# The order of VectorE's and ScalarE's steps in the projection and attention stages of a one-core encoder block

## The chip, the cores and the metric

The kernel runs on one core of a Trainium2 chip. The metric is device time in microseconds (us), the median of several runs. The core has five engines with a queue of instructions each: TensorE (PE; its weight loads are PEld), VectorE (DVE), ScalarE (ACT), GpSimd (POOL) and SyncE (SP, which issues most of the transfers). Each engine works through its own queue in the order of the program; the engines wait for one another through semaphores.

## The reference, cut to what matters

One layer of an encoder with 512 tokens and a width of 1024, in three residual blocks. Only the first block is touched by the change:

```python
xn = rms_norm(h, mix_norm[l])
q_a, k_a, v_a, q_b, k_b, v_b, q_i, k_i, w_i = jnp.split(xn @ w_in[l], IN_SPLITS, axis=-1)
# branch A: p = softmax of 4 heads x 2 maps; a = p[:, :, 0] - lam * p[:, :, 1]; o = a @ v
y_a = diff_attention(q_a, k_a, v_a, lam, slopes_a)
# branch B: isc = sum over 4 heads of relu(q_i k_i) * w_i; the 128 best keys of each query (top_k);
# softmax over these, 8 heads with one shared k_b, v_b
y_b = dsa_attention(q_b, k_b, v_b, q_i, k_i, w_i * ..., slopes_b, k_sel)
gates = jax.nn.sigmoid(xn @ w_gate[l] + b_gate[l])
h = h + (g_a * (y_a @ w_branch_a[l]) + g_b * (y_b @ w_branch_b[l])) @ w_out[l]
```

Behind it come cross attention over 256 memory tokens and a mixture of 32 experts, 2 for each token, whose weights are the larger part of all bytes that are read.

## The kernel before, in words

All five engines walk one list, `steps`, written out by hand near line 330; for each step an engine issues what that step gives it, and nothing if the step gives it nothing. Moving a step in the list moves its instructions in every engine's queue.

**Weights.** A weight matrix comes in chunks of at most 128x2048 numbers into a ring of three buffers `raw`. The step `("split", n)` turns chunk n into two parts: ACT copies it to `whi` (L904) once the chunk has landed and once PE has finished with chunk n-2, whose buffer it takes; DVE then writes the low part `wlo` = `raw` - `whi` (L1222). SP loads chunk n+3 when that low part is written. A step `("fm", n, j)` multiplies one half j of a chunk: 24 matmuls of 128x512 (L1647 to L1649: high x high, low x high, high x low, eight k). It waits for the low part of its chunk. Chunk 0 holds the keys of branch B and of the index (`CH_K`), chunk 1 `v_b` and `w_i` (`CH_VBWI`, 24 matmuls in the step `("vbwi",)`), chunk 2 the index queries (`CH_QI`). After `("fm", CH_K, 0)` ACT copies the keys out of PSUM (`kbT` L926, `kiT` L927) and issues two small transfers that double them to the other half of the partitions (L929, L930). The first reader of the doubled keys is the first step `("index", 1, 0)`, L1811 on PE.

**Selection.** The 128 best keys of each query come from 16 rounds for each of the query tiles 1, 2 and 3: a step `("topk", qt, r)` is one MAX (L1252) and one MATCH_REPLACE (L1253) on DVE. `select(n)` puts the next n of these steps into the list. Tile 3 must be through before unit 28 of the attention is scored.

**Attention.** Branch A is 16 units (4 query tiles x 4 heads), branch B 16 more (4 query tiles x 4 pairs of heads), 32 in all, u = 0 to 31. Each unit u has these steps:
- `("score", u)`: PE multiplies queries and keys (L1824), DVE adds the distance term (L1271) and takes the row maximum (L1273), for both maps;
- `("exp", u)`: ACT, softmax numerator and its sum (L976);
- `("fin", u)`: in branch A three instructions on DVE (L1282, L1283, L1286) that divide by the sums and subtract the two maps; in branch B one reciprocal on DVE (L1289) and two scalings on ACT (L984);
- `("tr", u)`: PE transposes the result (L1832), after waiting for `fin` of u; ACT copies it out of PSUM (L993);
- `("av", u)`: PE multiplies with the values (L1845 in branch A, L1850 in B); ACT and, in branch B, DVE copy out.

The loop over u puts down, for each u: `tr(u)`, `fin(u+1)`, `score(u+3)`, `exp(u+2)`, a `split` where u is a positive multiple of 4, twelve matmuls of a gate projection (`fm_half` or `fm`), `av(u)`, and perhaps `select(1)`. Ahead of the loop stand the two chunks `CH_QB` (the queries of branch B, chunks 9 and 10), with `fin(0)` and four selections each. PSUM has eight banks that are filled in turn; a step that fills a bank waits until the one before it is copied out.

Of the kernel before, what the change touches and what calls it, by code (L numbers as in the profile page):

```python
# [10 lines left out]
TT = SEQ // P  # L11
# [30 lines left out]
def build(nc, x, mem, mix_norm, w_in, lam_q1, lam_k1, lam_q2, lam_k2, diff_subln, w_branch_a, w_branch_b,  # L42
# [13 lines left out]
    def at(name, shape, dtype, start, offset=0):  # L56
        return nc.alloc_sbuf_tensor_at(name, shape, dtype, offset=start + offset)
# [33 lines left out]
    vbwi = at("vbwi", [DH_B + H_I, SEQ], f32, R_B)  # L91
# [177 lines left out]
    def fm_chunk(src, c0):  # L269

        chunks.append((256, [(src[:, :, c0:c0 + 256], 0, KT, 0, 256)]))
        return len(chunks) - 1
# [9 lines left out]
    CH_K = 0  # L282
    chunks.append((68, [(win[:, :, C_VB:C_VB + 64], 0, KT, 0, 64), (win[:, :, C_WI:C_WI + 4], 0, KT, 64, 4)]))
    CH_VBWI = 1
# [4 lines left out]
    CH_QB = [fm_chunk(win, C_QB + 256 * j) for j in (0, 1)]  # L289
# [25 lines left out]
    A_UNITS = [("A", qt, hd) for qt in range(TT) for hd in range(H_A)]  # L315
    B_UNITS = [("B", qt, pair) for qt in range(TT) for pair in range(H_B // 2)]
    UNITS = A_UNITS + B_UNITS
    steps = [("norm", "x"), ("cols",), ("split", 0)]
    steps += [("xT", k) for k in range(KT)] + [("split", 1)]

    def fm(n, js=(0, 1)):
        for j in js:
            steps.append(("fm", n, j))
        if n + 2 < NCH:
            steps.append(("split", n + 2))
# [7 lines left out]
        if n + 3 < NCH:  # L333
            steps.append(("split", n + 3))

    fm(CH_K, (0,))
    steps.append(("vbwi",))
    steps.append(("split", CH_VBWI + 2))
    steps += [("fm", CH_QI, 0), ("vbwiT",), ("fm", CH_QI, 1), ("split", CH_QI + 2), ("lambda",)]

    selecting = [("index", qt, hd) for qt in range(1, TT) for hd in range(H_I)]
# [2 lines left out]
    def select(n=2):  # L344
        steps.extend(selecting[:n])
        del selecting[:n]
# [14 lines left out]
    for n in CH_QB:  # L361
        steps.append(("fm", n, 0))
        if n == CH_QB[1]:
            steps.append(("fin", 0))
        select(2)
        steps.append(("fm", n, 1))
        steps.append(("split", n + 2))
        select(2)

    gate_tiles = [(CH_G[g // 2], g % 2) for g in range(2 * KT)]  # L370
    for u in range(len(UNITS)):
        steps.append(("tr", u))
        if u + 1 < len(UNITS):
            steps.append(("fin", u + 1))
        if u + 3 < len(UNITS):
            _, qt, _ = UNITS[u + 3]
            assert not any(q <= qt for _, q, _ in selecting) or UNITS[u + 3][0] == "A"
            steps.append(("score", u + 3))
        if u + 2 < len(UNITS):
            steps.append(("exp", u + 2))  # L380
        if u % 4 == 0 and u:
            steps.append(("split", CH_G[u // 4 - 1] + 2))
        if u < 2 * len(gate_tiles):
            n, j = gate_tiles[u // 2]
            steps.append(("fm" if u % 2 else "fm_half", n, j))
        steps.append(("av", u))
        if u < 2 * TT or u >= len(A_UNITS):
            select(1)
        if u == len(UNITS) - 2:

            steps.append(("yanorm",))
    n = CH_BR[0]
# [9 lines left out]
    n = CH_WO[1]  # L402
# [9 lines left out]
    n = CH_CV[1]  # L412
# [5 lines left out]
    for hx in range(1, H_X):  # L418
        n = CH_CQ[hx]
# [7 lines left out]
    n = CH_CO[0]  # L427
# [9 lines left out]
    steps = [s for s in steps if s[0] != "split" or s[1] < NCH]  # L437
# [10 lines left out]
    for s in steps:  # L448
# [15 lines left out]
        elif kind in ("score", "tr"):  # L464
            u = UNITS[s[1]]
# [1691 lines left out]
```

## Time and profile before

| | us |
|---|---|
| median of 3 runs | 1059.52 |
| lowest and highest | 1059.39, 1059.64 |
| the profiled execution's own time | 1057.06 |
| its span in the profile | 1055.3 |
| PE busy | 998.5 (95%) |
| DVE busy | 503.1 (48%) |
| ACT busy | 342.9 (32%) |
| PE's part of the chain that ended last | 80% |

The first stage (projections, both attentions, the gates) ends near 300 us, the cross attention near 560 us, the routing of the experts near 590 us; the experts take the rest. A row of the timeline has: start, duration, engine, line, operation, out<-in, shape, and in brackets the idle time of that engine before it with what ended it. Starts and durations are in us. The durations of instructions that follow one another overlap, so the pace of an engine is read from starts. ACTq and SPq are the engines' issues of transfers.

### The profile page before, as it was taken

The numbers are of one execution on the slowest core, as the hardware profiler recorded it, in microseconds if no ns is written. First come the engines' busy times: TensorE is split into PE (matmuls) and PEld (weight loads), VectorE is DVE, ScalarE is ACT, GpSimd is POOL, SyncE is SP. The second block draws the span as 40 slices with busy tenths as digits, with TensorE's granted clock in tenths as the row PEclk, the third lists the DMA queues.
The fourth block names the chain that finished last, engine by engine and source line by source line (L and its number), as shares of the span: only waits on it lengthen the run. The fifth ranks groups of instructions, "written<-read, shape, count | busy, mean of one in ns | idle before, by whom it ended". The sixth has DMA issues, their size and how long they took to land.

```text
span 1055.3 us, 12594 instructions
## 1 busy us (share of the span) xinstructions
PE 998.5 (95%) x4901; PEld 628.9 (60%) x4901; DVE 503.1 (48%) x915; ACT 342.9 (32%) x684; POOL 41.9 (4%) x59
## 2 busy tenths in 40 slices
PE   8999989989999999999997999999999889898894
PEld 6778857766778889887786444344443333333342
DVE  4369799766557545433336433333332232333236
ACT  6342346667872335443323211111111110111113
POOL 1000000000000000000000100000000000000001
PEclk9999999999999999999997999999999999999997
DMA  8322311211213525421287999999999999999992
GB/s 244 121 81 80 114 46 41 80 40 44 78 40 104 216 82 198 160 80 40 101 325 319 346 429 427 426 424 428 427 424 427 427 427 427 427 427 427 427 407 93
DMA packets 64431, 260.72 MB, mean 247 GB/s; under 512 B 11329, under 2 KB 39026, under 8 KB 50802
## 3 DMA queue, kind: packets, MB, share of 16 engines
q1 hardware_dynamic: 59954, 248.08, 59.3%
q0 software_dynamic: 3104, 7.35, 1.9%
q10 hardware_dynamic: 1312, 4.46, 1.1%
q8 instruction: 41, 0.67, 0.3%
q14 instruction: 20, 0.16, 0.0%
HBM read 259.60 MB, written 4.19 MB: 250 GB/s over the span
## 4 chain that ended last, share of the span: by engine, by line
PE 80%; DMA 13%; DVE 2%; issue 2%; ACT 2%; SPq 0%; DVEq 0%; ACTq 0%
PE ps L1956 16%; PE ps L1647 13%; PE ps L1649 13%; PE ps L1648 13%; DMA eraw<-in_w 12%; PE ps L2009 8%; PE ps L2020 2%; PE ps L1824 2%; PE ps L2021 2%; PE ps L1832 1%; PE ps L1882 1%; PE ps L1904 1%; PE ps L1850 1%; PE ps L1845 1%; PE ps L1943 1%
## 5 line engine op out<-in xcount | busy, mean ns | idle before, releaser
L1956 PE MATMUL ps<-eraw,XT 128*64 128x512 f32 x992 | 225.9, 598 | 12.8 <-DMA eraw<-in_w 11.6
L1222 DVE TENSOR_TENSOR wlo<-raw,whi 128x2048 fp32r<-128x2048 f32 (+2 forms) x43 | 95.9, 2230 | 120.0 <-ACT whi L904 119.8
L1956 PEld LDWEIGHTS ps<-eraw,XT 128*64 128x64 f32 x992 | 67.4, 137 | 133.6 <-issue 129.4
L2009 PE MATMUL ps<-eraw,HT 128*64 128x512 f32 x512 | 113.0, 594 | 8.0 <-issue 8.0
L1516 DVE TENSOR_TENSOR h<-ps,h 128x512 f32<-128x512 f32 x128 | 79.4, 682 | 82.9 <-PE ps L2021 82.9
L1647 PE MATMUL ps<-xT_hi,whi 128*128 128x512 f32 (+1 forms) x256 | 104.8, 409 | 2.8 <-DVE xT_lo L1229 1.6
L1648 PE MATMUL ps<-xT_lo,whi 128*128 128x512 f32 (+1 forms) x256 | 100.4, 392 | 0.0
L1649 PE MATMUL ps<-xT_hi,wlo 128*128 128x512 f32 (+1 forms) x256 | 100.2, 392 | 0.0
L904 ACT ACTIVATE whi<-raw 128x2048 fp32r<-128x2048 f32 (+2 forms) x43 | 80.1, 1863 | 44.7 <-PE ps L1649 43.2
L2009 PEld LDWEIGHTS ps<-eraw,HT 128*64 128x64 f32 x512 | 39.4, 137 | 79.7 <-issue 79.7
L1062 ACT ACTIVATE HT<-ps 128x512 f32<-128x512 f32 x15 | 9.0, 597 | 197.7 <-PE ps L1994 197.7
L1508 DVE TENSOR_TENSOR Yl<-ps,Yh 128x512 fp32r<-128x512 f32 x32 | 22.1, 691 | 96.7 <-ACT Yh L1081 96.7
L1647 PEld LDWEIGHTS ps<-xT_hi,whi 128*128 128x128 f32 (+1 forms) x256 | 47.9, 187 | 28.6 <-issue 15.0
L1525 DVE TENSOR_TENSOR gg<-ps,sg 128x512 f32<-128x512 f32 x16 | 11.1, 691 | 96.5 <-ACT sg L1090 94.5
L1649 PEld LDWEIGHTS ps<-xT_hi,wlo 128*128 128x128 f32 (+1 forms) x256 | 47.8, 187 | 11.0
L2020 PE MATMUL ps<-Yh,S 128*128 128x512 f32 x128 | 53.7, 420 | 0.3 <-DVE Yl L1508 0.3
L1648 PEld LDWEIGHTS ps<-xT_lo,whi 128*128 128x128 f32 (+1 forms) x256 | 48.1, 188 | 9.2
L1081 ACT ACTIVATE Yh<-ps 128x512 fp32r<-128x512 f32 x32 | 19.1, 597 | 100.7 <-PE ps L2009 100.7
L2021 PE MATMUL ps<-Yl,S 128*128 128x512 f32 x128 | 50.4, 394 | 0.0
L2020 PEld LDWEIGHTS ps<-Yh,S 128*128 128x128 f32 x128 | 24.0, 187 | 28.9 <-issue 23.9
L976 ACT ACTIVATE s<-s,nmax 128x128 f32<-128x128 f32 (+3 forms) x64 | 35.4, 560 | 1.0 <-DVE nmax L1273 0.6
L1090 ACT ACTIVATE sg<-ps 128x512 f32<-128x512 f32 x16 | 9.6, 597 | 77.0 <-PE ps L1956 77.0
(316 smaller groups left out, 1576.0 us busy)
## 6 DMA issues: line engine op xcount, KB each, us to landing
eraw<-in_w SPq DMA_DIRECT2D x82, 2048.0 KB, 29.1
eraw<-in_w SPq DMA_DIRECT2D x28, 1024.0 KB, 11.2
raw<-in_w_in SPq DMA_DIRECT2D x9, 1024.0 KB, 5.3
raw<-in_w_gate SPq DMA_DIRECT2D x8, 1024.0 KB, 5.4
raw<-in_w_ckv SPq DMA_DIRECT2D x8, 1024.0 KB, 5.2
raw<-in_w_out SPq DMA_DIRECT2D x4, 1024.0 KB, 5.0
raw<-in_w_cq SPq DMA_DIRECT2D x4, 1024.0 KB, 5.1
raw<-in_w_co SPq DMA_DIRECT2D x4, 1024.0 KB, 4.9
```

Source lines behind the costliest of these rows:

```text
L904: act.activation(whi[n % 2][:, 0:w], raw[n % RING][:, 0:w], ACT.Copy).then_inc(w_hi, 1)
L976: act.activation(b, b, ACT.Exp, bias=nmax[:, u % 3, m:m + 1], accum_out=ssum[:, u % 3, m:m + 1]).then_inc(exp_done, 1)
L1222: dve.tensor_tensor(wlo[n % 2][:, 0:w], raw[n % RING][:, 0:w], whi[n % 2][:, 0:w].bitcast(f32), ALU.subtract).then_inc(w_lo, 1)
L1508: dve.tensor_tensor(Yl[:, c], ps[4 + n][:, :], Yh[:, c].bitcast(f32), ALU.subtract).then_inc(yl_kept, 1)
L1516: dve.tensor_tensor(v, ps[bank][:, :], v, ALU.add).then_inc(comb_added, 1)
L1647: pe.matmul(o, ahi, bhi, start=start, stop=False)
L1648: pe.matmul(o, ahi, blo, start=False, stop=False)
L1649: return pe.matmul(o, alo, bhi, start=False, stop=stop)
L1956: ins = pe.matmul(ps[1 + c // 2][rows, :], XT[p % 2][:, kk, rows], eraw[slot][:, first + 512 * k:first + 512 * k + 512], start=(kk == 0), ...
L2009: ins = pe.matmul(ps[4 + n][rows, :], HT[:, ff, rows], eraw[slot][:, first + D * f + 512 * n:first + D * f + 512 * n + 512], start=(ff == ...
L2020: pe.matmul(o, S[:, P * t:P * t + P], Yh[:, c], start=True, stop=False)
L2021: pe.matmul(o, S[:, P * t:P * t + P], Yl[:, c], start=False, stop=True).then_inc(comb_made, 1)
```

## The change

Three things are edited in `steps`; no instruction is added or removed, and the memory layout is as before.

1. `("split", 2)` moves ahead of `("fm", CH_K, 0)`. (`CH_K + 2` and `CH_VBWI + 1` are both chunk 2; `CH_VBWI + 2`, chunk 3, stays behind `vbwi`.)
2. `("fin", 1)` moves from the loop's first pass to the chunk `CH_QB[1]`, behind its second half and ahead of `("split", 12)`.
3. The loop's `select(1)` used to stand in the units 0 to 7 and from 16 on. Now it stands in units that are no multiple of 4, up to 11 and from 16 on. The 11 rounds that are left for the loop (5 to 15 of tile 3) were in the units 0 to 7 and 16 to 18; they are now in 1, 2, 3, 5, 6, 7, 9, 10, 11, 17 and 18.

```diff
-    fm(CH_K, (0,))
-    steps.append(("vbwi",))
-    steps.append(("split", CH_VBWI + 2))
+
+    steps += [("split", CH_K + 2), ("fm", CH_K, 0), ("vbwi",), ("split", CH_VBWI + 2)]
...
         steps.append(("fm", n, 1))
+        if n == CH_QB[1]:
+            steps.append(("fin", 1))
         steps.append(("split", n + 2))
...
         steps.append(("tr", u))
-        if u + 1 < len(UNITS):
+        if 0 < u < len(UNITS) - 1:
             steps.append(("fin", u + 1))
...
         steps.append(("av", u))
-        if u < 2 * TT or u >= len(A_UNITS):
+
+        if u % 4 and (u < 3 * TT or u >= len(A_UNITS)):
             select(1)
```

On PE, POOL and SP no instruction changes its place. From here on the changed kernel's lines are 2 higher.

ACT's queue at the start of the projections, before: the keys (`kbT`, `kiT`) and their two transfers stand ahead of the copy of chunk 2 (`raw2` to `whi0`).

```order
L904 ACTIVATE whi1_53<-raw1_50 128x544
L926 ACTIVATE kbT_83<-ps1 64x512
L927 ACTIVATE kiT_84<-ps1 64x512
L929 DMA kiT_84<-kiT_84 64x512
L930 DMA kbT_83<-kbT_83 64x512
L904 ACTIVATE whi0_52<-raw2_51 128x2048
L952 ACTIVATE vbwi_78<-ps2 68x512
```

And the same place in the changed kernel:

```order
L906 ACTIVATE whi1_53<-raw1_50 128x544
L906 ACTIVATE whi0_52<-raw2_51 128x2048
L928 ACTIVATE kbT_83<-ps1 64x512
L929 ACTIVATE kiT_84<-ps1 64x512
L931 DMA kiT_84<-kiT_84 64x512
L932 DMA kbT_83<-kbT_83 64x512
L954 ACTIVATE vbwi_78<-ps2 68x512
```

The copy of chunk 2 has moved ahead of four instructions; on DVE the low part of chunk 2 keeps its place.

DVE's queue at the end of the chunk `CH_QB[1]` and the loop's first pass, before: the low part of chunk 12 (`wlo0`), two selection rounds, `fin(1)` (the three `rsum`, `s10` rows), `score(3)`.

```order
L1222 TENSOR_TENSOR wlo0_54<-raw0_49,whi0_52 128x2048
L1252 MAX top8_182<-work3_167 128x8
L1253 MATCH_REPLACE work3_167<-top8_182,work3_167 128x512
...
L1282 RECIPROCAL rsum_181<-ssum_180 128x2
L1283 TENSOR_SCALAR rsum_181<-rsum_181,neglam_173,ssum_180 128x1
L1286 SCALAR_TENSOR_TENSOR s10_155<-s11_156,rsum_181,s10_155 128x128
L1271 SCALAR_TENSOR_TENSOR s00_153<-dist_168,ps1 128x128
L1273 TENSOR_REDUCE nmax_179<-s00_153 128x1
```

In the changed kernel:

```order
L1284 RECIPROCAL rsum_181<-ssum_180 128x2
L1285 TENSOR_SCALAR rsum_181<-rsum_181,neglam_173,ssum_180 128x1
L1288 SCALAR_TENSOR_TENSOR s10_155<-s11_156,rsum_181,s10_155 128x128
L1224 TENSOR_TENSOR wlo0_54<-raw0_49,whi0_52 128x2048
L1254 MAX top8_182<-work3_167 128x8
L1255 MATCH_REPLACE work3_167<-top8_182,work3_167 128x512
...
L1273 SCALAR_TENSOR_TENSOR s00_153<-dist_168,ps1 128x128
L1275 TENSOR_REDUCE nmax_179<-s00_153 128x1
```

`fin(1)` has moved ahead of the low part and of both rounds.

DVE's queue in the pass u = 16, the first of branch B, before: the low part of chunk 16, the low part of the unit's output (`ybT_lo`), a selection round, and then the reciprocal of `fin(18)`.

```order
L1222 TENSOR_TENSOR wlo0_54<-raw1_50,whi0_52 128x2048
L1296 TENSOR_TENSOR ybT_lo_90<-ps5,ybT_hi_89 128x128
L1252 MAX top8_182<-work3_167 128x8
L1253 MATCH_REPLACE work3_167<-top8_182,work3_167 128x512
L1289 RECIPROCAL rsum_181<-ssum_180 128x2
```

In the changed kernel:

```order
L1224 TENSOR_TENSOR wlo0_54<-raw1_50,whi0_52 128x2048
L1298 TENSOR_TENSOR ybT_lo_90<-ps5,ybT_hi_89 128x128
L1291 RECIPROCAL rsum_181<-ssum_180 128x2
```

The round is gone from this place; in the same way it is gone from the passes 0 and 4, and there is one more in each of the passes 9, 10 and 11.

## Rows read from the trace of the kernel before

**Rows 1.** The page: the span of the profiled execution.
```profile
span 1055.3 us, 12594 instructions
```
**Rows 2.** PE's waits to 560 us: who waited for whom, total, times, longest.
```profile
PE ps L1832 <- DVE s L1286: 5.0, 1, 5.0
...
PE ps L1832 <- ACT gates L944: 2.1, 2, 1.1
```
**Rows 3.** Timeline, 20 to 29 us: ACT, DVE and PE around chunk 2.
```profile
21.76 0.59 ACT L926 ACTIVATE kbT<-ps 64x512 f32<-64x512 f32 x1 [2.67 <-PE ps L1649]
...
24.25 1.92 ACT L904 ACTIVATE whi<-raw 128x2048 fp32r<-128x2048 f32 x1 [1.30 <-issue]
...
26.20 2.29 DVE L1222 TENSOR_TENSOR wlo<-raw,whi 128x2048 fp32r<-128x2048 f32 x1 [5.13 <-ACT whi L904]
...
26.65 0.39 PE L1648 MATMUL ps<-xT_lo,whi 128*68 128x512 f32 x1
26.88 0.40 PE L1649 MATMUL ps<-xT_hi,wlo 128*68 128x512 f32 x1
28.55 0.50 PE L1647 MATMUL ps<-xT_hi,whi 128*128 128x512 f32 x1 [1.28 <-DVE wlo L1222]
```
**Rows 4.** Busy time by stretch; the last three columns: PE clock, DMA share, GB/s.
```profile
20.00:22.00 2.00, 2.00 (x10) 1.52 (x9) 1.07 (x2) 0.24 (x1) 0.00 (x0) 1.00 0.00 1
```
**Rows 5.** Timeline, 140 to 148 us: DVE and PE around tr(1) and tr(2).
```profile
140.04 0.69 DVE L1252 MAX8 top<-work 128x8 f32<-128x512 f32 x1
...
141.56 0.17 DVE L1282 RECIPROCAL rsum<-ssum 128x2 f32<-128x2 f32 x1
...
142.34 0.28 DVE L1271 SCALAR_TENSOR_TENSOR s<-dist,ps 128x128 f32<-128x128 f32 x1
142.47 0.48 PE L1832 MATMUL ps<-ident,s 128*128 128x128 f32 x1 [4.99 <-DVE s L1286]
...
143.37 0.68 DVE L1252 MAX8 top<-work 128x8 f32<-128x512 f32 x1
...
147.96 0.27 PE L1832 MATMUL ps<-ident,s 128*128 128x128 f32 x1
```
**Rows 6.** Busy time by stretch, columns as in rows 4, behind PE's long wait.
```profile
143.00:144.00 1.00, 1.00 (x4) 0.39 (x4) 0.97 (x3) 1.00 (x5) 0.00 (x0) 0.50 0.14 45
```
**Rows 7.** Timelines of DVE and PE, 160 to 205 us, the units 4 to 14.
```profile
160.64 2.29 DVE L1222 TENSOR_TENSOR wlo<-raw,whi 128x2048 fp32r<-128x2048 f32 x1 [1.52 <-ACT whi L904]
...
183.91 0.62 DVE L1286 SCALAR_TENSOR_TENSOR s<-s,rsum,s 128x384 f32<-128x384 f32 x1
...
184.58 0.55 PE L1832 MATMUL ps<-ident,s 128*128 128x128 f32 x3
...
196.34 0.69 DVE L1271 SCALAR_TENSOR_TENSOR s<-dist,ps 128x512 f32<-128x512 f32 x1 [0.56 <-PE ps L1824]
...
199.29 2.29 DVE L1222 TENSOR_TENSOR wlo<-raw,whi 128x2048 fp32r<-128x2048 f32 x1 [0.23 <-ACT whi L904]
...
199.98 0.60 PE L1832 MATMUL ps<-ident,s 128*128 128x128 f32 x4
...
201.50 0.16 DVE L1282 RECIPROCAL rsum<-ssum 128x2 f32<-128x2 f32 x1
...
204.68 0.60 PE L1832 MATMUL ps<-ident,s 128*128 128x128 f32 x4
```
**Rows 8.** Timeline, 220 to 225 us: DVE and PE around tr(18).
```profile
220.90 0.68 DVE L1252 MAX8 top<-work 128x8 f32<-128x512 f32 x1
...
222.40 0.17 DVE L1289 RECIPROCAL rsum<-ssum 128x2 f32<-128x2 f32 x1
...
224.69 0.33 PE L1832 MATMUL ps<-ident,s 128*128 128x128 f32 x1 [1.01 <-ACT gates L944]
```
**Rows 9.** Busy time by stretch, columns as in rows 4: routing and experts.
```profile
576.00:580.00 4.00, 3.96 (x27) 2.84 (x26) 3.57 (x12) 0.00 (x0) 0.34 (x1) 0.58 0.77 324
...
600.00:700.00 100.00, 100.00 (x466) 39.69 (x464) 32.29 (x51) 12.98 (x28) 5.84 (x6) 1.00 1.01 424
```

## The prediction, made before the changed kernel was run

> **What bounds the kernel now.** I read the page first, then PE's waits, then the timeline around each wait. PE is busy for 95% of the span of 1055.3 us [rows 1], so up to 560 us almost nothing but PE's own gaps can be won. The list of PE's waits shows the two large groups that this change is near [rows 2]: one of 5.0 us, a transpose of `tr` that waits for DVE's last instruction of `fin`, and 2.1 us in two waits for ACT's copies of the gates, of which one is 1.01 [rows 8]. The timeline adds a third, 1.28 us for the low part of chunk 2 [rows 3]. In the timeline the reader should see which instruction ended each wait, and what stood ahead of it in its engine's queue.
>
> One thing the list of waits hides. In the units 6 to 10 PE shows no wait, but `fin(10)` ends on DVE at 183.91 + 0.62 = 184.53 and PE's `tr(10)` starts at 184.58 [rows 7]. DVE, nearly always busy there, runs exactly at PE's heels: from the long wait to unit 10 both engines are the bound. A wait that PE loses ahead of that stretch is worth only what DVE can follow.
>
> **Edit 1, chunk 2 split earlier.** Before, ACT copies the keys at 21.76, issues two transfers, and starts the copy of chunk 2 at 24.25; DVE starts the low part at 26.20, 1.95 later, and PE goes on at 28.55 [rows 3]. After, the copy can start at 21.76, when the product of the keys is through: that product is what both wait for. It needs chunk 2 to have landed by then. From 20 to 22 us the transfers are idle, at 1 GB/s [rows 4], so all loads that were issued had landed. The low part starts at 21.76 + 1.95 = 23.71 and ends 2.29 later at 26.0. PE's last two matmuls of chunk 1 start at 26.65 and 26.88, a pace of 0.23, so the next one is due at 27.11 [rows 3]. The cover is 1.1 us, and PE doesn't wait. The first matmul behind the wait also took 0.50 instead of 0.40. Gain: 28.55 - 27.11 + 0.10 = 1.54, call it 1.55 us.
>
> What is pushed back: the two key copies and both transfers, by one copy of 1.92 us. Nobody needs them before the first index product, which PE reaches behind the 48 matmuls of chunk 2 and the 24 of the first half of chunk 3, over 14 us later. The copy of `vbwi` waits for PE anyway. On SP the load of chunk 5 waits for the low part of chunk 2 and comes 2.5 us sooner. I cost these at nothing. From here to 137 us PE shows no wait, and what DVE and ACT do there is released by PE through the banks, so the 1.55 us is carried whole.
>
> **Edit 2, `fin(1)` earlier, with the round of pass 0 gone.** Before, DVE did the low part of chunk 12, two rounds and then `fin(1)`; PE waited for 4.99 us, to 142.47 [rows 5]. After, `fin(1)` runs ahead of the low part, in a gap of 1.16 us in which DVE waited for ACT (its three instructions take 142.34 - 141.56 = 0.78), and `tr(1)` waits for nothing. But this isn't 5 us. The next bound is `fin(2)`: DVE has its two rounds done at 141.56 as before, then `score(3)`, 143.37 - 142.34 = 1.03, then `fin(2)`, 0.78 and some 0.13 to PE's start. So `tr(2)` starts at 143.5 instead of 147.96 [rows 5]: 4.46 us are won, and of the 5.0 us of waiting some 2.2 stay, ahead of `tr(2)`. PE's clock is part of this: behind the long wait it was granted at 0.50, the lower of its two levels, 1.2 GHz [rows 6], and pass 1 took 5.49 us (142.47 to 147.96). Pass 1 at the full clock is about 3.9 us, an estimate from its 12 matmuls at 0.23, its scores and its transposes; the low clock cost about 1.6 us.
>
> **Edit 3, the rounds.** One round is 141.56 - 140.04 = 1.52 us of DVE [rows 5]. The rounds of the passes 0 and 4 are gone, and three come in the passes 9, 10 and 11: by unit 14, DVE has one round more than before. Follow DVE to `fin(14)`, which started at 201.50 [rows 7]. From 141.56 on, `fin(1)` is gone (-0.78); DVE's idle times in between, 1.52, 0.56 and 0.23 [rows 7], were waits for ACT and PE, which are now ahead of it, and go (-2.31); one round is added (+1.52). New start: 201.50 - 0.78 - 2.31 + 1.52 = 199.93. `fin(14)` is 1.31 from its start to PE's, so `tr(14)` can't start before 201.24. PE by its own pace, with 4.46 won, would be at 199.98 - 4.46 = 195.52 with `tr(13)` and, 4.70 later, at 200.22 with `tr(14)`. DVE is later by 1.0 us: PE waits there, and of the 4.46 only 204.68 - 201.24 = 3.44 us is left. Behind unit 14 DVE has no rounds until unit 17, and PE leads again.
>
> In pass 16 a round of 1.52 (222.40 - 220.90) stood ahead of the reciprocal of `fin(18)` [rows 8]. ACT waited for that reciprocal and with it everything behind it in ACT's queue: two scalings, two exponentials, the copy of a gate tile out of the PSUM bank that the second transpose of `tr(18)` needs. That transpose started at 224.69; PE's two waits ahead of it, the last of 1.01 [rows 8], make 1.87. All of this comes sooner by the round: gain 1.50, and of the 1.87 some 0.4 remains. The other wait for the gates, of 1.1 [rows 2], is behind the last round, in pass 18, which stays: no gain.
>
> **The sum.** 1.55 + 3.44 + 1.50 = 6.5 us. Against the profiled execution's own time, 1057.06 (span 1055.3 and 1.8 around it), it gives 1050.6; the median of the runs lies 2.46 above that execution, so 1059.52 - 6.5 = **1053.0**. Is it carried to the end? From 240 us on nothing changes its order, and SP's loads are released by PE, DVE and ACT, not by the clock on the wall. In the experts both PE and the transfers are full, 100.00 of 100 us and 424 GB/s [rows 9]; the stream starts as much sooner as what releases it.
>
> **The rivals.**
>
> *Whole gain.* DVE's pace doesn't bind, because its gaps are larger than I read. Then the 4.99 us, the 1.6 us of low clock, 1.55 and 1.50 all count: 9.6 us, 1049.9. For it: the waits are real. Against it: rows 7 show `fin(10)` at PE's heels.
>
> *The added rounds cost in full.* If DVE keeps its idle times, 2.31 us, because ACT's copies for the splits stay late, then `tr(14)` is won by only 1.1 us: 1.55 + 1.1 + 1.50 = 4.2, 1055.3. For it: ACT's copy at unit 4 stands behind an exponential that needs DVE. Against it: that copy follows `tr(4)`, which comes 4 us sooner.
>
> *Taken back by the experts.* If the stream of expert weights keeps its own end, the 6.5 us turns into PE's waits for weights there: 1059.5, the same. For it: the stream is full. Against it: its first loads wait for products of the cross attention, and all of those shift.
>
> *Slower, by PE's clock.* In the routing stage PE idles, and the clock is at 0.58 on average from 576 to 580 us [rows 9]. If that low stretch ended later and reached into the experts, each us of it would cost 0.5 us, and there is no slack there to take it back [rows 9]. It decides from 13 us longer on, which cancels the 6.5; 18 us longer gives 1062. For it: the change shifts where the idle time falls against whatever times the clock. Against it: the work that leads up to it is the same. The 2.2 us that are left ahead of `tr(2)` are weighed by the same rows: behind the wait of 5.0 us the transpose took 0.48 [rows 5], behind the two waits ahead of `tr(18)`, 1.9 us together, it took 0.33 [rows 8], no sign of the low clock, and 2.2 is near the latter; at the worst it costs the 1.6 again.
>
> The Trainium skill (TensorE: Matmul & The Clock Gate, What's actually happening) says that the gate's timing runs freely and doesn't start with the kernel, so that the number of slow matmuls differs from run to run. By it the low stretches could come out otherwise by chance alone; the sum without the 1.6 us would be 4.9 instead of 6.5. The three runs of before lie within 0.25 us, which speaks against much of that.
>
> **How the numbers follow.** The sum as worked out has 0.62; the whole gain 0.10; rounds in full 0.14; taken back by the experts 0.09; slower by the clock 0.05. The range takes in the first three, 1049.5 to 1055.8, which is 0.86 of the chances. 0.2% is 2.1 us, about what a measurement of this kernel can tell from no change. Faster by more than that: 0.86; within: 0.09; slower: 0.05.
>
> **What would show it.** In the profile of the changed kernel: no wait ahead of the first matmul of chunk 2, near 27.1 us. `tr(1)` right behind `av(0)`. A wait of about 2.2 us for `fin(2)`, with the clock at 1.00 behind it, and one of about 1 us for `fin(14)`. DVE without idle time between them. The waits at `tr(18)` down from 1.9 to 0.4 us. Then the start of the experts 6.5 us sooner and the same length from there. I am wrong if the clock falls behind `tr(2)`, if DVE has gaps at the splits, or if the stretch from 240 us to the end is not as long as before.

## The result, and the profile after

The changed kernel took 1050.53 us (median of 4 runs, 1048.80 to 1051.55) against 1059.58 us for the kernel before (4 runs, 1059.39 to 1059.78): a ratio of 0.9908, with a 95% interval of 0.9894 to 0.9921, or 9.05 us less. The forecast was 1053.0, so 6.5 us less, and its range 1049.5 to 1055.8 holds the result. Two later sets of runs gave 1052.24 against 1060.39 (0.9929, 0.9904 to 0.9955) and 1051.38 against 1060.76 (0.9918, 0.9892 to 0.9943). The gain of the three sets is 8.2 to 9.4 us, so 1.7 to 2.9 us of it was not in the sum. The experiments are about these.

First the trace of the changed kernel, whose own time was 1051.55. Two rows of PE's waits up to 560 us, the same view as [rows 2] (who waited for whom, total, times, longest):

```profile
PE ps L1834 <- DVE s L1288: 3.1, 2, 2.0
...
PE ps L1834 <- ACT gates L946: 1.5, 2, 1.1
```

The 5.0 us have become 3.1 in two waits. The timeline of PE at `tr(2)`, `tr(14)` and the second transpose of `tr(18)` (the places of [rows 5], [rows 7] and [rows 8]):

```profile
142.00 0.33 PE L1834 MATMUL ps<-ident,s 128*128 128x128 f32 x1 [2.02 <-DVE s L1288]
...
199.51 0.66 PE L1834 MATMUL ps<-ident,s 128*128 128x128 f32 x4 [1.08 <-DVE s L1288]
...
218.09 0.33 PE L1834 MATMUL ps<-ident,s 128*128 128x128 f32 x1 [0.43 <-ACT gates L946]
```

The forecast had put `tr(2)` at 143.5 - 1.55 = 141.95 with a wait of 2.2, `tr(14)` at 201.24 - 1.55 = 199.69 with a wait of 1.0, and 0.4 us left at `tr(18)`. Chunk 2, in the timelines of ACT, DVE and PE (the place of [rows 3]):

```profile
21.96 1.92 ACT L906 ACTIVATE whi<-raw 128x2048 fp32r<-128x2048 f32 x1 [2.72 <-PE ps L1651]
...
23.91 2.29 DVE L1224 TENSOR_TENSOR wlo<-raw,whi 128x2048 fp32r<-128x2048 f32 x1 [2.68 <-ACT whi L906]
...
27.02 0.40 PE L1651 MATMUL ps<-xT_hi,wlo 128*68 128x512 f32 x1
27.25 0.39 PE L1649 MATMUL ps<-xT_hi,whi 128*128 128x512 f32 x1
```

PE goes from chunk 1 to chunk 2 without a wait, with 1 us to spare. And DVE, from its timeline: `fin(1)` fits ahead of the low part, which hardly waits any more, 0.18 us instead of 1.16:

```profile
133.77 0.17 DVE L1284 RECIPROCAL rsum<-ssum 128x2 f32<-128x2 f32 x1
...
134.81 2.29 DVE L1224 TENSOR_TENSOR wlo<-raw,whi 128x2048 fp32r<-128x2048 f32 x1 [0.18 <-ACT whi L906]
```

From 142 to 200 us DVE's timeline has no idle time at all: the three gaps of [rows 7] are gone.

To compare whole traces I use marks on PE: `tr(2)`, `tr(14)`, the second transpose of `tr(18)`, the 16 transposes of the last token tile for the router (L1695 before; "router" below), the first 32 matmuls of the experts, and the end of the span. The mark "router" is taken from the chain that ended last, the others from the timeline.

| | tr(2) | tr(14) | tr(18) | router | experts | span |
|---|---|---|---|---|---|---|
| before | 147.96 | 204.68 | 224.69 | 559.97 | 585.38 | 1055.3 |
| changed | 142.00 | 199.51 | 218.09 | 553.33 | 579.59 | 1049.8 |
| sooner by | 5.96 | 5.17 | 6.60 | 6.64 | 5.79 | 5.5 |

At `tr(18)` 6.60 us are won where the sum said 6.49, and at the router 6.64. Then 0.85 us is lost in the routing stage, and the experts take 470.2 instead of 469.9 us. So the pair of traces shows 5.5 us, and the medians 9. Both can't be the edits' doing alone.

The loss of 0.85 us goes with the place of a stretch of low clock, 13.7 us long in both traces, behind the router mark. It begins 5.7 us behind that mark before and 4.8 us behind it in the changed kernel, and so covers 4.1 us of PE's work there instead of 2.5. In all 14 traces of this document it begins 4.8 to 7.2 us behind the mark, and the earlier it begins, the longer the routing stage takes: 26.2 to 26.3 us where it begins at 4.8 and 5.0, 25.4 at 5.7, and 24.3 to 24.4 from 7.0 on.

### The profile page after: what moved, and what is told of

Read it like the earlier page. It is cut to its first block, busy times and chain, and to the rows that moved or that the text cites. A ratio compares the mean times of both kernels' runs of the same rounds, so it can differ in the third digit from the quotient of the medians.

```text
span 1049.8 us, 12592 instructions
## 1 busy us (share of the span) xinstructions
PE 997.7 (95%) x4901; PEld 629.3 (60%) x4901; DVE 503.1 (48%) x915; ACT 343.2 (33%) x684; POOL 41.9 (4%) x59
## 4 chain that ended last, share of the span: by engine, by line
PE 75%; DMA 13%; DVE 6%; issue 3%; ACT 1%; SPq 0%; DVEq 0%; POOLq 0%
PE ps L1958 16%; DMA eraw<-in_w 12%; PE ps L1649 12%; PE ps L1650 12%; PE ps L1651 12%; PE ps L2011 8%; PE ps L2022 2%; PE ps L2023 2%; PE ps L1884 1%; PE ps L1906 1%; PE ps L1826 1%; PE ps L1834 1%; DVE s L1273 1%; DVE nmax L1275 1%; PE ps L1852 1%
```

## The experiments

**A second trace of the kernel before.** No edit.

> The kernel before, unchanged, for a second trace. In the trace of before PE's clock is at its lower level for 3.4 us behind the wait ahead of tr(1) and 13.7 us in the routing stage. Theory A (stretches of low clock fall differently from execution to execution, and the one that was traced, at 1057.06, had fewer than most of the runs near 1059.9): a trace of an execution near 1060 shows 6.8 us instead of 3.4 behind tr(1), or a further 3.4 us behind tr(18), and the marks behind it 1.5 to 3 us later than in the first trace. Theory B (the difference lies in the expert stage): the marks up to 558 us are those of the first trace, and the experts take 2.5 us more.

Measured: 1060.44 (8 runs, 1057.53 to 1061.87); its kernel is the one before, at 1060.39 in the same set. The traced execution took 1061.87, 4.8 us more than the first trace. Its timeline, PE at `tr(1)`, `tr(2)`, `tr(14)` and twice at `tr(18)`:

```profile
142.89 0.47 PE L1832 MATMUL ps<-ident,s 128*128 128x128 f32 x1 [4.99 <-DVE s L1286]
...
149.73 0.27 PE L1832 MATMUL ps<-ident,s 128*128 128x128 f32 x1
...
206.48 0.60 PE L1832 MATMUL ps<-ident,s 128*128 128x128 f32 x4
...
225.16 0.33 PE L1832 MATMUL ps<-ident,s 128*128 128x128 f32 x1 [0.85 <-ACT s L984]
226.50 0.33 PE L1832 MATMUL ps<-ident,s 128*128 128x128 f32 x1 [1.01 <-ACT gates L944]
```

The wait is the same 4.99 us, but pass 1 took 6.84 us (142.89 to 149.73) instead of 5.49. The cause stands in the busy time by stretch (its length, the busy us of PE, PEld, DVE, ACT and POOL with their instructions, then PE's mean granted clock, the share of the transfers, GB/s). The first trace of before, from 140 to 152 and from 216 to 234 us:

```profile
140.00:152.00 12.00, 9.53 (x36) 6.76 (x37) 11.30 (x34) 3.47 (x14) 0.00 (x0) 0.86 0.25 83
216.00:234.00 18.00, 15.89 (x80) 10.25 (x79) 13.27 (x31) 9.49 (x32) 0.00 (x0) 1.00 0.18 59
```

The second trace of before, the same stretches:

```profile
140.00:152.00 12.00, 9.11 (x28) 6.31 (x29) 10.68 (x31) 3.33 (x14) 0.00 (x0) 0.72 0.28 87
216.00:234.00 18.00, 16.13 (x76) 10.77 (x75) 11.12 (x27) 9.70 (x34) 0.00 (x0) 0.91 0.18 59
```

The clock has two levels, so a mean of 0.86 over 12 us is 12 x 0.14 x 2 = 3.4 us at the lower level, 1.2 GHz, and 0.72 is 6.7. A mean of 0.91 over 18 us is another 3.2 us, behind `tr(18)`, where the first trace had none. Read in the same way from stretches of 1 us in every trace, the low stretches came out as 3.4, 6.8, 10.2 or 13.7 us long; a last one runs into the end of the span in all 14 traces, 9.0 to 11.9 us of it within the span. The router is reached at 563.32, 3.35 us later than in the first trace. This speaks for theory A of this run in the main: the first trace of before, on which the prediction rests, was of an execution with less low clock than most. The clocks of the single runs say so too: of the 61 later runs of this kernel, nine had a mean granted clock of 0.986, as the traced execution had, or more, and took 1057.22 us in the median; the other 52, at 0.982 to 0.985, took 1060.24. The experts began 3.33 us later and took 1.5 us longer, so some of the difference is theirs, as theory B had it, by an amount that I can't explain.

**Each edit alone.** Edit 1:

```diff
-    fm(CH_K, (0,))
-    steps.append(("vbwi",))
-    steps.append(("split", CH_VBWI + 2))
+    steps += [("split", CH_K + 2), ("fm", CH_K, 0), ("vbwi",), ("split", CH_VBWI + 2)]
```

> Edit 1 alone (the split of chunk 2 ahead of the keys' copies), everything else as before. Theory A, the pace theory of the prediction: the first matmul of chunk 2 starts near 27.1 us, and all later marks up to 550 us come 1.55 us sooner: tr(1) at 140.9, tr(14) at 203.1, tr(18)'s second transpose at 223.1, the last router stage's first product at 556.7. What the medians show beyond 1.55 us is the routing stage's clock, up to 2.5 us either way. Theory B: the 9 us that the changed kernel won are all made by the edits, in proportion, so edit 1 gives 1.55 x 9.05/6.6 = 2.1 us in every run.

Measured: 1058.49 (10 runs) against 1059.87 (25 runs), ratio 0.9992 (0.9980 to 1.0005), which by itself is no proof of anything. The traces say more. This one has the low stretches of the second trace of before (6.8 us behind `tr(1)`, 3.4 behind `tr(18)`), so that is its partner: `tr(18)` at 224.96 against 226.50, router at 561.75 against 563.32. That is 1.54 and 1.57 us; the sum said 1.55. So close a match is in part luck: the two traces of before are 0.4 us apart already at `tr(0)` (133.62 and 134.04), ahead of all these low stretches. But there all 14 traces can be compared: `tr(0)` starts at 133.56 to 134.04, median 133.67, in the five without edit 1, and at 131.94 to 132.51, median 132.13, in the nine with it, 1.54 us sooner. Against the first trace of before, which lacks 6.8 us of low clock, edit 1 would look 1.8 us slower at the router. The marks in my expectation were worked from that trace, and so they missed.

Edit 2:

```diff
         steps.append(("fm", n, 1))
+        if n == CH_QB[1]:
+            steps.append(("fin", 1))
         steps.append(("split", n + 2))
...
-        if u + 1 < len(UNITS):
+        if 0 < u < len(UNITS) - 1:
             steps.append(("fin", u + 1))
```

> Edit 2 alone (fin(1) ahead of chunk 12's low part), the selection rounds as before. Theory A: tr(1) right behind av(0) at 137.3; then DVE does score(3), the round of pass 0 and fin(2), so tr(2) starts at 145.0 (before 147.96). DVE has lost fin(1) (0.78) and its idle time at unit 4 (1.52), so tr(10) comes 2.3 us sooner, at 182.3, and tr(14) at 202.4. The wait at tr(18) stays. Gain up to 550 us: 2.3. Theory B, whole gain: PE keeps the 5.0 us of the wait and 1.6 us of low clock, gain 6.6.

Measured: 1056.66 (10 runs), ratio 0.9973 (0.9960 to 0.9987), 3.2 us less. PE at `tr(2)`, in its timeline:

```profile
145.01 0.33 PE L1834 MATMUL ps<-ident,s 128*128 128x128 f32 x1 [3.54 <-DVE s L1288]
```

`tr(2)` at 145.0 is as worked out: `fin(2)` behind one more round is the next bound, and of the 5.0 us of waiting 3.5 stay. But the clock fell behind this wait too (0.86 from 140 to 152 us), pass 2 took 5.55 us, and so `tr(14)` came at 202.84, 1.84 us sooner and not 2.3. It fell once more behind the full wait at `tr(18)`, so that the router, at 559.78, is only 0.2 us sooner than in the first trace of before and 3.5 sooner than in the second. The whole gain of 6.6 (theory B) is out: the next wait is there, 3.54 us long.

Edit 3:

```diff
-        if u < 2 * TT or u >= len(A_UNITS):
+        if u % 4 and (u < 3 * TT or u >= len(A_UNITS)):
             select(1)
```

> Edit 3 alone (no rounds in the passes 0, 4 and 16, one more in each of 9, 10, 11); fin(1) stays in pass 0. Theory A: PE's wait of 5.0 us ahead of tr(1) stays, with the low clock behind it, tr(2) stays near 147.9; DVE is 1.5 us sooner from there, PE gains up to 0.5 in the units 3 to 10, where it was at DVE's heels; the three added rounds put fin(14) on the path, tr(14) at 204.5 to 205.0 (before 204.68); tr(18) loses 1.5 of its 1.9 us of waiting. Gain up to 550 us: 1.2 to 1.7. Theory C, the rounds cost in full: three rounds of 1.52 and none saved, 3 us slower at tr(14), 1.5 us slower in all.

Measured: 1058.07 (10 runs), ratio 0.9986 (0.9974 to 0.9998), 1.8 us less. In the trace the low stretch behind `tr(1)` is of the longer kind, 6.8 us; `tr(2)` came at 149.09, `tr(14)` at 206.04 with a wait of 0.36 for DVE, and `tr(18)` at 224.61. The second trace of before has the same 6.8 us behind `tr(1)`, but is 0.5 us later already at `tr(1)` (142.89 against 142.41), which edit 3 doesn't touch. Counted from `tr(1)`, edit 3 gives nothing at `tr(14)` and 1.4 us at `tr(18)` (1.9 less 0.5), where 1.9 us of waits have become 0.4; the low stretch behind them is missing too. The added rounds don't cost in full (theory C).

The three edits alone give 1.4 + 3.2 + 1.8 = 6.4 us by the medians, together 8.2 to 9.4. A part of the surplus is the order itself: the round of pass 0 stands behind `fin(1)` and ahead of `fin(2)`, so taking it out pays at `tr(2)` only with edit 2 beside it. Edit 2 alone has `tr(2)` at 145.01, 143.5 if the 1.55 of edit 1 is taken off; all three have it at 142.00, 1.5 us sooner. The rest fits the clock: each edit alone keeps a wait of 3.5 us or more, all three leave none over 2.1. No run separates the two parts.

**PE kept busy in the waits, kernel before.** DVE and ACT have the same instructions in the same order.

```diff
                     br, qt, _ = UNITS[u]
+                    for key, n in {1: [(("tr", 1, 0), 14)], 18: [(("tr", 18, 0), 3)]}.get(u, ()):
+                        o = opened(*key)
+                        for _ in range(n):
+                            pe.matmul(o[:, 0:P], ident[:, :], ident[:, :], start=True, stop=True)
                     pe.wait_ge(fin_done, u + 1)
```

> The kernel before with PE kept busy in its waits: 14 matmuls of the identity (128x128) ahead of the wait for fin(1), into the bank that tr(1) fills next, and 3 ahead of that for fin(18). Nothing else is changed, DVE and ACT are as before. Theory A: the wait ahead of tr(1) ends at the same 142.4, but no low clock behind it, nor behind tr(18). tr(2) comes 1.6 us sooner than in the first trace of before, at 146.4; DVE is the bound at units 6 to 10, so that tr(10) stays at 184.5. The median falls from 1059.9 to some 1057.0, the level of the executions with few stretches, and with it the spread up to there. Theory B (the clock costs nothing there): median within 0.5 of before.

Measured: 1056.76 (10 runs, 1054.91 to 1059.41) against 1060.39 (20 runs), ratio 0.9967 (0.9952 to 0.9981): 3.6 us less, by matmuls whose results nobody reads. The timeline of PE:

```profile
137.44 3.29 PE L1831 MATMUL ps<-ident 128*128 128x128 f32 x28
142.56 0.33 PE L1836 MATMUL ps<-ident,s 128*128 128x128 f32 x1 [1.83 <-DVE s L1286]
```

(The trace has two records for each of these matmuls.) `tr(1)` waits for DVE until 142.56, as before, and the median falls to where the first trace of before stood (1057.06). What differs is the clock: 0.9863 on average over the 10 runs, 0.9842 over the 20 beside them. That is 4.5 us less at the lower level, worth 2.3 us, an estimate at half a microsecond for each; what made the other 1.3 is not shown. The detail was half wrong: behind `tr(1)`, where 1.83 us of idle time was left, the clock still fell for 3.4 us, only not for 6.8; behind `tr(18)` it stayed up. One more stretch of 3.4 us, at 932 us, lies in the experts. Marks are within 0.15 us of the first trace of before: `tr(2)` 148.08, router 560.11.

**PE kept busy at tr(2), changed kernel**, five such matmuls ahead of `tr(2)`.

```diff
+                    for key, n in {2: [(("fm", CH_G[0], 1), 5)]}.get(u, ()):
+                        o = opened(*key)
+                        for _ in range(n):
+                            pe.matmul(o[:, 0:P], ident[:, :], ident[:, :], start=True, stop=True)
```

> The changed kernel with 5 matmuls of the identity ahead of tr(2), in the wait of 2.0 us, into the bank of the gate tile that comes next. Theory A: the marks stay as in the trace of the changed kernel (tr(2) at 142.0, within 0.1), as the clock was at its upper level there anyway; the median moves by less than 0.5 us, or down by up to 1 if some executions had a low stretch there. Theory C (what is left of waiting costs 2 us and more through the clock): 2 us less.

Measured: 1050.92 (4 runs, 1050.17 to 1051.86). The marks are those of the changed kernel, no low stretch ahead of the router (553.45). In the wait 0.89 us of idle time is left. Beside the next run's 1052.24 that is 1.3 us less, but with intervals that overlap; I take it as no more than a hint.

**The changed kernel, twice more.** No edit.

> The changed kernel, unchanged, for a second trace and more runs. Theory A: its longest wait up to 550 us is 2.0 us, behind which the clock falls seldom; marks as in the first trace, no low stretch ahead of 550 us in most executions; runs from 1048.5 to 1051.7 with the median near 1050.5, 9 us below before. Theory B (the first four runs were lucky): the median comes back to 1059.9 - 6.6 = 1053.3.

> The changed kernel, unchanged, beside the next three on one chip. Theory A: median 1050.5 to 1052.3, 8 to 9 us below before; a low stretch of 3.4 us ahead of 550 us in some executions (behind tr(20) in the second trace), none in others.

Measured: 1052.24 (5 runs, 1049.36 to 1054.14) and 1051.38 (4 runs, 1051.04 to 1052.89). Both traces hold one low stretch of 3.4 us that the first lacked: one behind `tr(20)` (a wait of 1.12 us), router at 554.84, 1.5 us later than in the first; the other behind `tr(2)`:

```profile
141.95 0.33 PE L1834 MATMUL ps<-ident,s 128*128 128x128 f32 x1 [2.02 <-DVE s L1288]
147.55 0.27 PE L1834 MATMUL ps<-ident,s 128*128 128x128 f32 x1
...
200.07 0.66 PE L1834 MATMUL ps<-ident,s 128*128 128x128 f32 x4 [0.37 <-DVE s L1288]
```

Here pass 2 took 5.60 instead of 4.03 us, but the wait for DVE at `tr(14)` shrank from 1.08 to 0.37: where DVE is the bound, a part of the low clock is hidden, and the router, at 554.00, is only 0.67 us later than in the first trace. The expectation of no low stretch in most executions doesn't hold: two traces of three have one. Theory B, a gain of 6.6 us alone, is a ratio of 0.9938, which both intervals here still hold and the first set's doesn't. Taken together, 13 runs of the changed kernel have a mean of 1051.5 and 61 of the kernel before 1059.9: 8.5 us, give or take 0.9 (two standard errors), and 6.6 is out.

**One round back in pass 16**, taken from pass 9.

```diff
-        if u % 4 and (u < 3 * TT or u >= len(A_UNITS)):
+        if u in (1, 2, 3, 5, 6, 7, 10, 11, 16, 17, 18):
             select(1)
```

> The changed kernel with one round moved back from pass 9 to pass 16, where it stood before. Theory A: DVE has one round less by unit 14, so the wait ahead of tr(14), 1.08 us, goes; the waits at tr(18) are back, 1.9 us instead of 0.4; by the marks 0.4 us later than the changed kernel at tr(18). Behind it the clock falls for 3.4 us in most executions, as in three of the four traces of kernels that have this wait in full, which costs 1.5 more: median 2 us above the changed kernel. Theory B (the clock costs nothing there): 0.4 above.

Measured: 1052.86 (5 runs, 1051.65 to 1055.07) beside 1051.38 of the changed kernel, 1.5 us more, with intervals that overlap. The trace:

```profile
198.16 0.63 PE L1834 MATMUL ps<-ident,s 128*128 128x128 f32 x4
...
216.87 0.33 PE L1834 MATMUL ps<-ident,s 128*128 128x128 f32 x1 [0.86 <-ACT s L986]
218.22 0.33 PE L1834 MATMUL ps<-ident,s 128*128 128x128 f32 x1 [1.01 <-ACT gates L946]
```

and its stretch from 216 to 234 us:

```profile
216.00:234.00 18.00, 14.90 (x66) 9.87 (x64) 11.30 (x31) 11.35 (x36) 0.00 (x0) 0.91 0.16 55
```

`tr(14)` no longer waits, the waits at `tr(18)` are back, and by the marks the two nearly cancel: `tr(18)` at 218.22 against 218.09. The router, though, is reached at 555.19 against 553.33: behind the returned waits the clock fell for 3.4 us, and that costs 1.7 of the 1.86.

**The last rounds later.** None in the passes 9, 10, 11 and 18.

```diff
-        if u % 4 and (u < 3 * TT or u >= len(A_UNITS)):
-            select(1)
+        select({1: 1, 2: 1, 3: 1, 5: 1, 6: 1, 7: 1, 13: 1, 14: 1, 15: 2, 17: 1}.get(u, 0))
```

> The changed kernel with its last five rounds moved: none in the passes 9, 10, 11 and 18, but one in 13 and 14, two in 15, one in 17. Theory A: DVE has some 10 us of idle time in the passes 13 to 16, so these rounds are hidden there; PE's wait of 1.08 us ahead of tr(14) goes, and the wait of 1.12 us ahead of tr(20) too, since the last round with its two closing instructions no longer stands ahead of fin(20). 2.2 us less than the changed kernel up to 550 us, 8.8 less than before. Theory D: DVE is no bound at unit 14, the wait there has another cause: then the waits stay and the marks don't move, or the two rounds in pass 15 delay tr(17) by up to 1.5.

> The kernel with the last five rounds in the passes 13, 14, 15, 15 and 17 again, for more runs. Theory A: 2.2 us less than the changed kernel by the marks and in the median, near 1048.5 to 1050, as tr(14) and tr(20) wait for nothing; the only low stretches left are the one in the routing stage and now and then one behind the wait of 2.0 us ahead of tr(2).

Measured: 1048.46 (4 runs, 1046.68 to 1050.21) against 1059.87, and 1049.84 (4 runs, 1046.40 to 1051.75) against 1060.76. The latter is 1.5 us less than the 1051.38 of the changed kernel beside it, with intervals that overlap; the marks are clearer. The waits of PE from 100 to 540 us in the second trace:

```profile
PE ps L1833 <- DVE s L1287: 2.0, 1, 2.0
...
PE ps L1833 <- ACT gates L945: 0.4, 1, 0.4
```

The waits at `tr(14)` and `tr(20)` are gone; the five rounds are hidden. The router is at 550.54 in this trace, 2.79 us ahead of the changed kernel's first, and 552.20 in the first trace, where the clock fell behind `tr(2)` for 3.4 us. Theory D is out.

**And the two rounds ahead of tr(2) moved too.**

```diff
         steps.append(("split", n + 2))
-        select(2)
+        if n == CH_QB[0]:
+            select(2)
...
-        if u % 4 and (u < 3 * TT or u >= len(A_UNITS)):
-            select(1)
+        select({1: 1, 2: 1, 3: 1, 5: 1, 6: 1, 7: 1, 9: 1, 10: 1, 13: 1, 14: 1, 15: 2, 17: 1}.get(u, 0))
```

> As the kernel with late rounds, and the two rounds behind the low part of chunk 12 moved as well, to the passes 9 and 10. Theory A: fin(2) is ready 3.0 us sooner, the wait of 2.0 us ahead of tr(2) goes, tr(2) at 139.9, all marks from there 2.0 us sooner; DVE is 1 us further ahead, so that the two rounds in 9 and 10 are hidden and tr(14) doesn't wait. 4.2 us less than the changed kernel, 2.0 less than the late rounds; no wait over 0.5 us from unit 0 to unit 25 and so no low stretch ahead of the routing stage: median near 1046.5. Theory D (ACT's queue or a PSUM bank is the next bound): under half of it, and new waits for ACT in the list.

Measured: 1045.20 (4 runs, 1044.21 to 1047.44) against 1060.76, ratio 0.9860 (0.9833 to 0.9888): 6.2 us less than the changed kernel beside it, and the fastest of all. PE's waits from 100 to 540 us, all of them:

```profile
PE ps L1649 <- issue: 0.8, 1, 0.8
PE ps L1834 <- ACT gates L946: 0.4, 1, 0.4
```

and its stretch from 140 to 152 us, where PE is busy throughout at the upper level:

```profile
140.00:152.00 12.00, 12.00 (x55) 8.88 (x55) 11.37 (x31) 7.98 (x27) 0.00 (x0) 1.00 0.12 43
```

`tr(2)` is at 139.55, the router at 548.56, 4.8 us ahead of the changed kernel's first trace where 4.2 were worked out. No low stretch stands ahead of the routing stage. The one in it is 10.2 us long, not 13.7, and begins 7.0 us behind the router mark; the stage takes 24.4 us from mark to mark, against 26.3 in the first trace of the changed kernel. It is the later beginning that goes with the shorter stage: with 10.2 us beginning at 6.5 (PE kept busy, kernel before) it takes 24.8, with 13.7 beginning at 6.4 (PE kept busy at `tr(2)`) 25.1. Whether the order of the rounds moves that beginning, or chance does, is not shown.

## Why the prediction was right, and where it was short

- **Edit 1**: right. 1.54 us at `tr(0)` over all traces, against 1.55. The keys' copies and transfers, 2 us later, delayed nothing.
- **Edit 2**, with the round of pass 0 gone: right in mechanism and size. `tr(1)` stopped waiting and DVE's `fin(2)` was next; `tr(2)` at 142.00 against 141.95 by the sum, with 2.02 us of waiting left where I said 2.2. A pass 1 at the full clock takes 3.90 us (135.65 to 139.55, in the last run above), as estimated. A reader who takes the 5.0 us of the list of waits as the gain is wrong by 2.
- **Edit 3**: right. DVE's rate bound `tr(14)`: at 199.51 with a wait of 1.08, worked out 199.69 and 1.0. The wait at `tr(18)` went from 1.87 to 0.43.
- **The stretch up to the router**: 6.64 us in the pair of first traces, 6.49 by the sum.
- **The step that was short** is the sentence "the median of the runs lies 2.46 above that execution, so 1059.52 - 6.5". I carried that difference over as if it were a constant. It was mostly low clock: the traced execution had 3.4 us of it ahead of the routing stage, the second trace, at 1061.87, 10.2. The sum's term for the low clock, 1.6 us behind `tr(1)`, is thus that of one favourable execution; in the second trace pass 1 took 2.9 us more than its 3.9, and the stretch behind `tr(18)` another 1.5 (from there to the router 336.8 us instead of 335.3). The change shortens the waits behind which this clock falls: over all runs the mean granted clock went from 0.9841 (61 runs) to 0.9872 (13), which is 6.7 us less at the lower level, worth 3.4 us where the sum had 1.6. That estimate covers 1.8 of the 1.7 to 2.9 us that were missing; it counts PE's idle time as if it were work, and so is rough. Filling the waits with idle matmuls gave 3.6 us of median with no edit to the order.
- **Luck**: the range holds the result because its lower end was set by the whole gain, 1049.9, whose mechanism is out.
- **Where I weighed the clock** I said that behind waits of 1.9 us there is no sign of the low clock, from one trace. That was wrong. Behind the full wait at `tr(18)`, 1.9 us, it fell in four traces of five (the second trace of before, edits 1 and 2 alone, and the round in pass 16), behind the 2.0 us at `tr(2)` in two of six, behind the 1.12 us at `tr(20)` in one of eleven. The Trainium skill (TensorE: Matmul & The Clock Gate, What's actually happening) says that the gate's timing runs freely and the number of slow matmuls varies from run to run. The second half is borne out by these traces: the same kernel, 3.4 and 10.2 us ahead of the routing stage; what times the gate, no run here shows. I discounted it because three runs lay within 0.25 us; of 25 runs in the next set, five were below 1058 and the others spread to 1061.2.
- **The rivals**: the whole gain of 9.6 us has nearly the right total and the wrong reason; the marks show 6.6, not 9.6. The rounds in full are out, as `tr(14)` and DVE's timeline show. The gain taken back by the experts is out: they took 470.2 us against 469.9. The slower rival had the right place, but its mechanism, a stretch that ends later and reaches into the experts, didn't occur: the low stretch was 13.7 us in both first traces, began and ended 0.9 us sooner behind the router mark, and that went with a loss of 0.85 us.

What stays open: why the experts take 469.5 to 471.6 us from trace to trace, what decides whether the clock falls behind a wait of 1 to 2 us, and where the stretch in the routing stage begins.

## What to carry to other kernels

When a wait is removed, work out when the same instruction's next wait would end on the other engine: here 5 us of waiting, with 1.6 us of low clock behind them, were worth 4.4 at `tr(2)` and 3.6 at `tr(14)`, because VectorE's work was the next bound. Put filler work where the busy engine has idle time, not evenly; moving five and then seven selection rounds into such places gave a further 1.5 us (2.8 by the marks) and 6.2 us. A wait of TensorE may cost more than its length: look at the granted clock behind it in more than one trace, and don't treat the gap between a profiled execution and the median as a constant.

## What the runs showed of the hardware

Behind waits of TensorE of 1.1 to 5.0 us, with dense work on both sides, the granted clock fell to its lower level for stretches of 3.4 us or 6.8 us; behind the shorter waits it did so in some executions of a kernel and not in others. One such stretch of 3.4 us in full work delays the marks by 1.5 to 1.7 us (router at 554.84 against 553.33, 552.20 against 550.54). It has a large part in the spread of an unchanged kernel on one core, 1056.58 to 1062.45 us over 61 runs: the nine with a mean granted clock of 0.986 or more have a median of 1057.22, the others of 1060.24. In an unchanged order 17 idle matmuls lowered the median by 3.6 us.

A low stretch of 10.2 or 13.7 us stands in the routing stage in every trace. Its beginning matters more than its length: 4.8 us behind the router mark the stage took 26.3 us, 7.0 us behind it 24.4.
